# GpSimd multiplies and square sums in the norm closings of a four-layer float32 kernel, and two more PSUM banks after them

## The reference

```python
# stages 0 to 3: retention, conv_ffn 0, differential attention, conv_ffn 1
h = mixer(rms_norm(x, pre_gain))        # ends in ... @ w_out
x = x + rms_norm(h, post_gain)
def rms_norm(x, g):
    return x * rsqrt(mean(x * x, axis=-1) + 1e-6) * g
# stages 4 to 7: conformer conv, conv_ffn_2, sparse attention, conv_ffn_2
x = x + mixer(rmsnorm(x, g))
```

## Time and profile before

| | |
|---|---|
| median of 3 runs | 2878.49 us (2877.47 to 2881.68) |
| the profiled execution, its own time | 2882.15 us |
| its span, first to last instruction | 2880.4 us |
| PE busy | 2762.9 us (96%) |
| PE weight loads | 2088.3 us (73%) |
| DVE busy | 1657.2 us (58%) |
| ACT busy | 1192.4 us (41%) |
| POOL busy | 151.2 us (5%) |
| mean granted TensorE clock | 0.985 of 2.4 GHz |
| DMA | 229 MB, 80 GB/s on average |

### The profile page before, as it was taken

How to read it: one execution, slowest core, us unless ns; L and a number is a source line. 1 busy time by engine, 2 the same in 40 slices (tenths; PEclk the granted TensorE clock), 3 DMA queues, 4 the chain that set the end, 5 groups by cost and what they waited for, 6 DMA issues and landing times.

```text
span 2880.4 us, 34171 instructions
## 1 busy us (share of the span) xinstructions
PE 2762.9 (96%) x11775; PEld 2088.3 (73%) x11775; DVE 1657.2 (58%) x2294; ACT 1192.4 (41%) x1927; POOL 151.2 (5%) x141
## 2 busy tenths in 40 slices
PE   8999998999989988999989989999988999999999
PEld 6777776888867656888866657888866555788887
DVE  4444426776254755777338955554366787555532
ACT  4333324444243544444336654333234666433321
POOL 0000000000000000000005710000000222000000
PEclk9999999999999999999999999999999999999999
DMA  4222232333322112333321213333333000233322
GB/s 144 75 77 76 73 95 66 96 93 93 93 77 88 52 38 72 95 95 89 93 81 52 61 42 95 95 95 90 95 95 105 22 16 23 74 95 95 95 88 95
DMA packets 419614, 229.26 MB, mean 80 GB/s; under 512 B 7939, under 2 KB 411468, under 8 KB 419404
## 3 DMA queue, kind: packets, MB, share of 16 engines
q1 hardware_dynamic: 418172, 225.18, 26.6%
q10 hardware_dynamic: 1360, 3.02, 0.3%
HBM read 226.07 MB, written 2.10 MB: 79 GB/s over the span
## 4 chain that ended last, share of the span: by engine, by line
PE 82%; DVE 9%; ACT 5%; issue 2%; POOL 1%; DMA 0%; DVEq 0%; ACTq 0%; POOLq 0%
PE lin L751 21%; PE lin L753 21%; PE lin L752 21%; DVE con_a L2404 2%; PE stat L767 1%; DVE w_both L1946 1%; PE lin L1052 1%; PE att L896 1%; PE att L860 1%; PE att L859 1%; PE att L861 1%; ACT w_both L1363 1%; PE att L1013 1%; ACT n_pt L1658 1%; PE lin L1079 1%
## 5 line engine op out<-in xcount | busy, mean ns | idle before, releaser
L1946 DVE TENSOR_TENSOR w_both<-raw,w_both 128x1024 fp32r<-128x1024 f32 x427 | 527.8, 1236 | 642.0 <-ACT w_both L1363 627.9
L1363 ACT ACTIVATE w_both<-raw 128x1024 fp32r<-128x1024 f32 x427 | 452.2, 1059 | 770.9 <-PE lin L753 685.6
L751 PE MATMUL lin<-xh,w_both 128*128 128x512 f32 x1856 | 742.0, 400 | 5.5 <-DVE w_both L1946 5.1
L753 PE MATMUL lin<-xh,w_both 128*128 128x512 f32 x1856 | 734.5, 396 | 0.0
L752 PE MATMUL lin<-xl,w_both 128*128 128x512 f32 x1856 | 734.4, 396 | 0.0
L751 PEld LDWEIGHTS lin<-xh,w_both 128*128 128x128 f32 x1856 | 348.9, 188 | 99.7 <-issue 14.6
L752 PEld LDWEIGHTS lin<-xl,w_both 128*128 128x128 f32 x1856 | 348.9, 188 | 86.8 <-issue 2.9
L753 PEld LDWEIGHTS lin<-xh,w_both 128*128 128x128 f32 x1856 | 348.7, 188 | 85.1
L752 PE MATMUL lin<-ffn_lo,w_both 128*128 128x512 f32 x704 | 279.1, 396 | 0.0
L751 PE MATMUL lin<-ffn_hi,w_both 128*128 128x512 f32 x704 | 279.1, 396 | 0.0
L753 PE MATMUL lin<-ffn_hi,w_both 128*128 128x512 f32 x704 | 279.1, 396 | 0.0
(11 more groups left out here) (370 smaller groups left out, 3780.9 us busy)
## 6 DMA issues: line engine op xcount, KB each, us to landing
raw<-in_ffn_w_up SPq DMA_DIRECT2D x176, 512.0 KB, 3.8
raw<-in_ffn_w_down SPq DMA_DIRECT2D x64, 512.0 KB, 3.6
raw<-in_a_w_in SPq DMA_DIRECT2D x48, 512.0 KB, 3.8
raw<-in_ffn_w_down SPq DMA_DIRECT2D x32, 384.0 KB, 3.1
raw<-in_conv_w_pw SPq DMA_DIRECT2D x24, 512.0 KB, 3.9
raw<-in_nsa_w_in SPq DMA_DIRECT2D x21, 512.0 KB, 3.7
raw<-in_a_w_out SPq DMA_DIRECT2D x16, 512.0 KB, 3.6
raw<-in_w_kv SPq DMA_DIRECT2D x16, 512.0 KB, 3.8
```

The source lines that it names most:

```text
L751: pe.matmul(bank, w_hi[s][:, k, :], h, start=start and k == 0, stop=False)
L753: done = pe.matmul(bank, w_lo[s][:, k, :], h, start=False, stop=stop and k == kc - 1)
L1363: act.activation(w_hi[s][:, :, :], raw[s][:, :, :], ACT.Copy).then_inc(hi_done[s], 1)
L1946: dve.tensor_tensor(w_lo[s][:, :, :], raw[s][:, :, :], w_hi[s][:, :, :].bitcast(F32), ALU.subtract).then_inc(lo_done[s], 1)
```

## The change

It does the following, for all four closings unless a closing is named.

- The post gain is multiplied in by ACT, as the scale of its copy to `hT`; DVE's y is then a plain multiply of two SBUF tiles.
- ACT squares each output and copies it before it splits the next weights. Inside the last unit of the last output, PE sums the seven squares in `acc`; after that unit it adds the eighth square alone. The eighth copy to `hT` comes after `rs`.
- A and C: POOL multiplies chunks 2 to 7 by `rs` in place (`SCALED_ALL`), D: chunks 2, 4 and 6 (`SCALED_SOME`), B: none. DVE adds these straight to x, without a y. The order of DVE is y0, x0, y1, xl0, x1, x2, xl1, x3, xl2 and so on.
- A and C: the squares of the new x go to a tile of their own, `x_sq`, in eight chunks. POOL adds 0+1, 2+3, these two, and 4+5; DVE adds 6+7 and the 4+5; PE sums two tiles into `stat` rather than eight. LAG is 2, not 4. Both weight splits for units 2 and 3 come before `rs_x`, and units 2 and 3 go to two banks of `att` rather than `lin`.
- B: the first square of x is written straight to `acc`, which needs no clearing.
- Some semaphores with the same use are merged.

```diff
-LAG = 4
+SCALED_ALL = (2, 3, 4, 5, 6, 7)
+SCALED_SOME = (2, 4, 6)
+LAG = 2
+        x_sq = Map().place("x_sq", [P, DC, T])
 # gpsimd
+            def scale_closing(hT, chunks):
+                pool.wait_ge(rs_ready, rss.next())
+                for c in chunks:
+                    if c == DC - 1:
+                        pool.wait_ge(h_ready, closes.last())
+                    pool.tensor_tensor(hT[:, c, :], hT[:, c, :], rs[:, :], ALU.mult).then_inc(h_scaled, 1)
+            def add_squares():
+                e = entries.next() - 1
+                pool.wait_ge(xsq_ready, e * DC + 2)
+                pool.tensor_tensor(x_sq[:, 0, :], x_sq[:, 0, :], x_sq[:, 1, :], ALU.add).then_inc(xsq_first, 1)
+                pool.wait_ge(xsq_ready, e * DC + 4)
+                pool.tensor_tensor(x_sq[:, 2, :], x_sq[:, 2, :], x_sq[:, 3, :], ALU.add).then_inc(xsq_first, 1)
+                pool.wait_ge(xsq_first, e * 4 + 2)
+                pool.tensor_tensor(x_sq[:, 0, :], x_sq[:, 0, :], x_sq[:, 2, :], ALU.add).then_inc(xsq_first, 1)
+                pool.wait_ge(xsq_ready, e * DC + 6)
+                pool.tensor_tensor(x_sq[:, 4, :], x_sq[:, 4, :], x_sq[:, 5, :], ALU.add).then_inc(xsq_first, 1)
 # tensor, beside(): after chunk(0, c) and chunk(1, c - lag)
-                        if sums:
-                            sum_square(c == 0, c == DC - 1)
+                    if beyond is not None:
+                        beyond(c - DC + 1)
 # tensor, closing
+            def closed(hi, lo, kcs, outputs, fresh=None):
+                def earlier_squares():
+                    ...
+                    pe.wait_ge(sq_used, squares.last())
+                    pe.matmul(stat[:, :], c_("ones"), acc[:, :], start=True, stop=False).then_inc(sum_done, 1)
+                project(hi, lo, kcs, outputs - 2, fresh)
+                output(hi, lo, kcs)
+                output(hi, lo, kcs, inside=earlier_squares)
+                sum_square(False, True)
 # tensor, ffn()
+                    def square_sums(late):
+                        if late == 0:
+                            pe.wait_ge(xsq_first, 4 * e - 1)
+                            pe.matmul(stat[:, :], c_("ones"), x_sq[:, 0, :], start=True, stop=False)
+                        if late == LAG:
+                            pe.wait_ge(xsq_rest, 2 * e)
+                            pe.matmul(stat[:, :], c_("ones"), x_sq[:, 6, :], start=False, stop=True).then_inc(sum_done, 1)
+                    beside(xh, xl, lambda k: (xl_ready, first_ + k + 1), LAG, square_sums)
+                    for u in range(2):
+                        unit(att[:, u, :], xh, xl, 0, UC, True, True)
 # scalar, project_out()
-                    for n in range(nu):
+                    for n in range(nu - 1):
                         split_next(no_more and o * nu + n >= 2 * nu - 2)
+                    s, t = multiplied()
                     b, _t = banks.take()
                     square(lin[b][:, :])
-                    act.activation(hT[:, k, :] ..., lin[b][:, :], ACT.Copy).then_inc(bank_free[b], 1)
+                    act.activation(hT[:, at(k), :], lin[b][:, :], ACT.Copy, scale=col(gain, k + g0)).then_inc(bank_free[b], 1)
+                    split(s, t, ...)
 # vector, project_out()
-                    dve.scalar_tensor_tensor(y[c % 2][:, :], hT[:, c, :], col(gain, g0 + c), rs[:, :], ALU.mult, ALU.mult).then_inc(t_ready, 1)
+                    dve.tensor_tensor(y[c % 2][:, :], hT[:, c, :], rs[:, :], ALU.mult).then_inc(t_ready, 1)
+                for c in range(DC):
+                    if c != 1 and c not in scaled:
+                        update(c)
+                    if c in scaled:
+                        dve.wait_ge(h_scaled, scaled_h.next())
+                        dve.tensor_tensor(x[:, c, :], x[:, c, :], hT[:, c, :], ALU.add).then_inc(x_ready, 1)
+                    elif then is not None or normed is not None:
+                        dve.wait_ge(t_ready, upd_t.last())
+                        dve.tensor_tensor(x[:, c, :], x[:, c, :], y[c % 2][:, :], ALU.add).then_inc(x_ready, 1)
+                    if c == 0:
+                        update(1)
+                    if then is not None and c != 1:
+                        low(max(c - 1, 0))
+                if then is not None and not summed:
+                    dve.wait_ge(xsq_ready, e * DC)
+                    dve.tensor_tensor(x_sq[:, 6, :], x_sq[:, 6, :], x_sq[:, 7, :], ALU.add).then_inc(xsq_rest, 1)
+                    dve.wait_ge(xsq_first, 4 * e)
+                    dve.tensor_tensor(x_sq[:, 6, :], x_sq[:, 6, :], x_sq[:, 4, :], ALU.add).then_inc(xsq_rest, 1)
 # scalar, ffn() of kind 1
-                    act.wait_ge(sq_used, squares.last())
+                    split_next()
+                    split_next()
+                act.wait_ge(sum_done, accs.next())
                 inverse_rms(D, dst=rs_x)
-                    split_next()
```

More of the change, by code:

```diff
@@ L1386, in gained_x, with project_out @@
                 pre.next()
-                square(x[:, at(c), :], apart=not isinstance(c, int))
-            def project_out(hT, nu, final=False, then=None, first=0, between=(), table=True, normed=False):
+                if apart:
+                    act.activation(x_sq[:, c, :], x[:, c, :], ACT.Square).then_inc(xsq_ready, 1)
+                else:
+                    square(x[:, at(c), :], apart=not isinstance(c, int), dst=dst)
+            def project_out(hT, nu, gain, g0, final=False, then=None, first=0, between=(), table=True, normed=False, summed=False):
@@ L1391, in project_out, with last_unit @@
                 if table:
                     act.preload_act_table_set(LN)
[L1394 to L1399 removed]
+                def last_unit(o, no_more):
+                    for n in range(nu - 1):
+                        split_next(no_more and o * nu + n >= 2 * nu - 2)
+                    s, t = multiplied()
+                    b, _t = banks.take()
+                    square(lin[b][:, :])
+                    return s, t, b
@@ L1405, in project_out @@
                     for o in range(2):
                         one(o, i * 2 + (o + first), False)
-                if final:
-                    for o in range(2):
-                        one(o, DC - 2 + o, True)
+                one(0, DC - 2, final)
+                s, t, b = last_unit(1, final)
+                split(s, t, final)
                 act.wait_ge(sum_done, accs.next())
+                act.wait_ge(sq_used, squares.last())
                 inverse_rms(D)
+                act.activation(hT[:, DC - 1, :], lin[b][:, :], ACT.Copy, scale=col(gain, DC - 1 + g0)).then_inc(h_ready, 1)
@@ L1974, in add_square, with project_out, one @@
                 dve.tensor_tensor(acc[:, :], acc[:, :], sq[(squares.n - 1) % 2][:, :], ALU.add).then_inc(sq_used, 1)
-            def project_out(hT, nu, gain, g0, final=False, then=None, first=0, between=(), summed=False, normed=None):
+            def project_out(hT, nu, final=False, then=None, first=0, between=(), summed=False, normed=None, scaled=()):
                 dve.memset(acc[:, :], 0.0).then_inc(acc_zero, 1)
                 zeros.next()
-                def one(o, no_more):
-                    for n in range(nu):
+                def one(o, no_more, last=False):
+                    for n in range(nu - 1):
                         split_next(no_more and o * nu + n >= 2 * nu - 2)
-                    add_square()
+                    if last:
+                        squares.next()
+                    else:
+                        add_square()
+                    split_next(no_more and o * nu + nu - 1 >= 2 * nu - 2)
                 dve.wait_ge(acc_zero, zeros.last())
@@ L1987, in project_out @@
                     one(o, False)
-                n_loop = (DC - first) // 2 - (1 if final else 0)
-                with rounds(dve, n_loop, (units, 2 * nu), (squares, 2)):
+                with rounds(dve, (DC - first) // 2 - 1, (units, 2 * nu), (squares, 2)):
                     for o in range(2):
                         one(o, False)
-                if final:
-                    for o in range(2):
-                        one(o, True)
+                one(0, final)
+                one(1, final, last=True)
                 for _ in range(DC):
@@ L1997, in project_out, with update @@
                 dve.wait_ge(rs_ready, rss.next())
-                for c in range(DC):
+                closes.next()
+                def update(c):
                     n = upd_t.next()
@@ L2561, in ffn, with pair @@
                 width = 2 * FC if kind == 1 else FC
-                def pair(i):
+                def pair(i, own=lin, splits=(0, 1), produced=None):
                     n = f_n.next()
```

225 lines of the change are left out of this document (118 added, 107 removed).

## The result

Median of 16 runs each: before 2878.56 us (2875.8 to 2884.31), changed 2886.18 us (2883.25 to 2887.61), ratio 1.0024 (95% 1.0018 to 1.003). The change costs 5.2 to 8.6 us by the ratio, where the forecast was +0.7. That is inside the range of 2859 to 2888, but it is the outcome "slower" (given 0.22) and not "same" (0.49): with +6.9 by the ratio and +7.6 by the medians it lies past the 5.8 us that I called no change.

A forecast was written before the change was run, and what follows sets the result against it. PE's standing still or working for nothing, longest in the closings, was taken as the bound. A and C +4.7, B -3.0, D -1.0 summed to +0.7 on the median 2878.5: 2879.2 us, range 2859 to 2888.

The forecast's parts named there:

- Head: Start of all four closings: 3.10 us from new E to DVE's start; A and C gain 2.54 each, B 1.96, D 2.22.
- POOL beside DVE: Middle of A and C: POOL and DVE exclude each other, 1.14 us per POOL instruction; middle 22.6 against 16.87, +5.7.
- Rival 1: Closings A, C, D: POOL and DVE do not exclude each other; -19 us, 2859.5 us; chance 0.09.
- rival 2: Middle of A and C: exclusion for tensor_tensor alone, `xl` passes; -8.2, 2870 us; chance 0.17.
- Rival 3: A, C and D: each POOL instruction costs more than in the conformer, 0.3 more each; +7.6, 2886 us; chance 0.14.
- Rival 4: Middle of A and C: PE stays at half clock, closings 7.0 later each; +14.7, 2893 us; chance 0.06.
- Tail of A and C: From last `xl` to unit 2: 5.15 us against 5.97, -0.8; splits of units 2 and 3 covered.
- The two banks only take back this wait: Units 2 and 3 in A and C: own banks avoid some 2.2 us of PE standing that LAG 4 lacked; costed at nothing.
- B: Closing B, without POOL: head 1.96 and each `xl` 1.0 earlier; -3.0 us.
- D: Closing D: head -2.22, middle and square-sum backlog +1.2; net -1.0, from -2.6 (no exclusion) to +0.5 (half clock throughout).
- The loops: Projection outputs: last unit's split moves 1.1 us later, covered with 2.2 to spare; no cost.

The follow-up runs named there:

- Run 2: The changed kernel with the weight split of the feed-forward's second pair moved to that pair's first half; ratio 1.0015 to the kernel before.
- run 5: On top of run 4: rs_x made between ScalarE's two weight splits, ffn_hg likewise on VectorE, second pair's split in its first half; ratio 0.9986 to the kernel before.
- run 8: The changed kernel with units 2 and 3 back in the two common banks, only the first pair ahead of the loop; ratio 1.0044 to the kernel before.
- run 4: The changed kernel without GpSimd in any closing: VectorE scales all chunks, TensorE sums eight squares one by one in A and C; ratio 0.9996 to the kernel before.
- 7: On top of run 5 with the Silu table loaded later: VectorE adds squares 4+5 and 6+7 after its last xl; ratio 0.9971 to before, median 2869.95 us.

## Why the prediction was right in part and wrong in part

- **Head: right.** 3.10 predicted, 3.29 in all four closings; the shift of E by 0.86 shows in the distances. The passes over the square ran near full clock (1.13, where half clock had taken 2.08).
- **POOL beside DVE: right, and the deciding price.** Six multiplies at 1.71 to 1.76, x, y and `xl` at 1.63 to 1.77 beside them. The middle was 22.6 by the sum and 22.41 in the trace. By the Trainium skill ("SBUF — State Buffer", section "Who interferes with whom") a VectorE instruction with two SBUF inputs contends with a GpSimd instruction that reads SBUF. I had written that the section names no operation; it does name tensor_tensor, but not scalar_tensor_tensor. This trace now agrees for multiplies and for scalar_tensor_tensor (1.75 against 0.75), on which the trace of before was silent. Rival 1 falls, and so does rival 2, which needed an `xl` of 0.74 beside POOL. Rival 3 falls as well: its time (+7.6) is by chance that of the medians, but POOL's durations stayed under 1.8. Rival 4's premise came true in part and its price didn't: in A the granted clock was 0.50 from 452.4 to 463.5, where the kernel before was at 0.92 from 454 on, yet it was full for the tail, and unit 2 came at E' + 30.45. C did the same at a clock of 0.64 from 1127 to 1130 (E' + 30.47). The `xl` of DVE set the pace.
- **Tail of A and C: the failed step.** Up to unit 2 it holds: 5.15 predicted, in A 4.75 and then the 0.39 that the last sum still costs behind unit 2's start; unit 2 at old E + 31.31 against 31.7. (The old tail has one sum of squares behind the last `xl`, at 465.82, not two as I wrote; its length of 5.97 is right.) But I wrote that "the splits of units 2 and 3 end before PE wants them" and costed the own banks at nothing. The splits do, but the next one, in the slot of unit 3, stands in the second half of the second pair, and that pair follows the first, which starts 2 us into unit 2. PE stands 1.15 ahead of unit 5, whose lateness makes 1.30 start to start, then 0.23 at unit 6 and 0.11 at unit 7: 1.63 in each closing, where I had nothing. I followed the units to the bank but not the slot to its next use. Run 2 takes 1.1 of it away in each by moving only that split. Without GpSimd the lateness was 2.47, and run 5 brought it to 0.56 by moving the split and rs_x; no run ends the last 0.56.
- **"The two banks only take back this wait": half right.** By run 8 they bring unit 2 forward by 2.96 (I had 2.2 for the standing, which was 2.39) and cost 1.6 in the later waits.
- **B: right.** -3.0 predicted, -2.80 in the distance from B to C.
- **D: mis-sized.** -1.0 predicted, +0.13 measured at the end of the second unit (35.67 after E' against 36.40 after E, with 0.86 for the sum). The last x was right (11.5 after DVE's start, predicted 11.7), the backlog of square sums was not: it ended 4.3 past the last x and not 2.6, at half clock for longer. It lay within my ends of -2.6 and +0.5.
- **The loops: no cost shown.** In these nine profiles with the new heads E' of A lies at 442.25 to 443.70, where 442.39 would be no cost; the changed one's 443.25 is inside that scatter. So the 0.86 there is not shown to be the change's, and is not explained.

Against +0.7 the spans give +5.4: the waits behind unit 2 3.3 more than forecast over A and C (1.63 each), D 1.1, B 0.2, the start 0.9, less 0.8 behind D, which is well within the 5 us that two executions differ there. The medians give 7.6, and the interval of the ratio reaches from 5.2 to 8.6.

So why does a change slow the kernel whose head is shorter by 3.2 in A and C, 2.6 in B and 2.9 in D? Of these 11.9 it pays back 3.4 for the sums inside the last units. GpSimd makes the middle of A and C 5.7 longer each against a VectorE alone (22.41 against 16.71 in run 4); since it spares TensorE six sums, 3.5 of it is left at unit 2 (30.45 against 26.91). The late pair costs 1.6 in each. Run 4 with the two splits in the right places (5) keeps the head and is faster than before; with TensorE relieved by VectorE's idle end (7) it is clearly so (0.9971, at most 0.9981).

## What to carry to other kernels

Work given to GpSimd beside a VectorE that reads two SBUF tiles was not parallel (1.63 to 1.77 for an instruction of 0.69 to 0.75): compare what the instruction holds on GpSimd (an estimate of 1.14 here) with what it saves on VectorE (0.70) before moving it. Work that saves VectorE nothing is dearest: here the four additions of squares lengthened the middle by 4.2, the six multiplies by 1.5. When a buffer is doubled or a result put aside, follow every resource that the old wait kept in step, the weight slots and the order of splits above all, to its next two uses. And an engine's idle end of a stretch (VectorE behind its last xl) was here a better place for reductions than GpSimd beside a busy VectorE.

## What the runs showed of the hardware that I had not expected

- A pause of TensorE of 2.0 to 2.4 us in the middle of full work was followed in one closing by 3.4 to 4.2 us mostly at half clock (run 8 in A, 2.39 and a clock of 0.59; run 4 in C, 1.98 and 0.51) and in the other closing of the same kernel by none. The loss was some 1.5 us in run 8 and 1.3 us in run 4 on top of the pause, and the profile of one execution doesn't say how often it comes.
- In D something alike happened on a small scale: three multiplies of GpSimd delay VectorE's last x by only 0.78, yet D's second unit ends 2.5 later (35.67 against 33.21). The square sums came apart, and TensorE worked them off at 0.50.
